# Feed-forward input product by Strassen's seven block products from the fourth slab on

## The reference, cut to what matters

```python
D_FF = 2816
h = x @ w_ffn_in                  # (512, 1024) @ (1024, 2 * 2816)
gate, up = split(h)
x = layer_norm(ALPHA * x + (silu(gate) * up) @ w_ffn_out)
```

## Time and profile before

| what | value |
|---|---|
| median of three runs | 3310.77 us |
| profiled execution, its own time | 3321.89 us |
| its span, first to last instruction | 3320.1 us |
| mean granted TensorE clock | 0.974 of full |
| PE busy | 3131.1 us (94%) |
| DVE busy | 1383.3 us (42%) |
| ACT busy | 1096.3 us (33%) |
| POOL busy | 340.4 us (10%) |

### The profile page before, as it was taken

The page is one execution under the profiler, slowest core; times in us unless marked ns, Lnnn a source line. Parts: engine busy times, 40 slices in busy tenths (PEclk is TensorE's granted clock), DMA queues, the critical chain, the costliest instruction groups (busy, mean ns, idle before and its releaser), DMA issues.

```text
span 3320.1 us, 37603 instructions
## 1 busy us (share of the span) xinstructions
PE 3131.1 (94%) x14830; PEld 2232.9 (67%) x14830; DVE 1383.3 (42%) x1859; ACT 1096.3 (33%) x1831; POOL 340.4 (10%) x266
## 2 busy tenths in 40 slices
PE   6989999979998979999999999998999999999998
PEld 3867777853433338775777688886776677868886
DVE  5676354350211144545334533334554433543333
ACT  3245332231111124455333322213445533232222
POOL 2456020010000001111110000000211110000000
PEclk8988999989999999999999999999999999999999
DMA  6011433448999971110123132233111112322222
GB/s 224 26 51 51 166 138 114 161 194 359 421 421 421 421 247 64 64 53 32 64 70 101 64 102 89 86 92 92 64 52 40 52 63 77 101 77 89 97 84 73
DMA packets 241679, 436.72 MB, mean 132 GB/s; under 512 B 9696, under 2 KB 180192, under 8 KB 216160
## 3 DMA queue, kind: packets, MB, share of 16 engines
q1 hardware_dynamic: 241504, 434.32, 36.2%
HBM read 432.19 MB, written 2.10 MB: 131 GB/s over the span
## 4 chain that ended last, share of the span: by engine, by line
PE 57%; DVE 3%; ACT 2%; DVEq 1%; issue 0%; DMA 0%; ACTq 0%; SPq 0%
PE bank L2314 47%; PE bank L2375 2%; PE bank L2392 2%; PE bank L2411 1%; PE bank L2351 1%; PE bank L1950 1%; DVE ring_r L2644 1%; PE bank L2381 1%; PE bank L2406 1%; ACT ring_r L2511 1%; DVE layers_norm_rstd L1982 1%; DMA ring<-in_w_in 0%; PE bank L2289 0%; DVE layers_negmax L2678 0%; DVEq L2679 0%
## 5 line engine op out<-in xcount | busy, mean ns | idle before, releaser
L2314 PE MATMUL bank<-experts_x_hi_r,ring_r 128*128 128x512 f32 x1720 | 577.4, 401 | 7.0 <-DVE ring_r L2644 7.0
L2314 PE MATMUL bank<-x_r,ring_r 128*128 128x512 f32 x1376 | 546.3, 397 | 0.0
L2644 DVE TENSOR_TENSOR ring_r<-ring,ring_r 128x2048 fp32r<-128x2048 f32 (+2 forms) x162 | 324.4, 2003 | 421.9 <-ACT ring_r L2511 420.7
L2511 ACT ACTIVATE ring_r<-ring 128x2048 fp32r<-128x2048 f32 (+2 forms) x162 | 272.5, 1682 | 477.2 <-PE bank L2314 456.7
L2314 PEld LDWEIGHTS bank<-experts_x_hi_r,ring_r 128*128 128x128 f32 x1720 | 324.3, 189 | 109.9 <-issue 25.7
L2314 PE MATMUL bank<-ring_r 128*128 128x512 f32 (+1 forms) x1224 | 387.5, 377 | 0.0
L2314 PE MATMUL bank<-layers_work_r,ring_r 128*128 128x512 f32 x1312 | 387.0, 396 | 0.0
L2314 PEld LDWEIGHTS bank<-x_r,ring_r 128*128 128x128 f32 x1376 | 259.1, 188 | 63.4 <-issue 1.4
L2823 POOL TENSOR_TENSOR layers_p<-layers_p,layers_recip 128x512 f32<-128x512 f32 (+2 forms) x160 | 145.1, 923 | 1509.2 <-DVEq L2688 1509.2
L2314 PEld LDWEIGHTS bank<-layers_work_r,ring_r 128*128 128x128 f32 x1312 | 245.8, 187 | 68.0 <-issue 7.9
L2314 PEld LDWEIGHTS bank<-ring_r 128*128 128x128 f32 x1224 | 223.7, 188 | 46.7
(11 more groups left out here) (412 smaller groups left out, 4826.4 us busy)
## 6 DMA issues: line engine op xcount, KB each, us to landing
ring<-in_w_in SPq DMA_DIRECT2D x74, 1024.0 KB, 5.1
ring<-in_w_ffn_in SPq DMA_DIRECT2D x44, 1024.0 KB, 5.0
mixer_kept<-in_w_up SPq DMA_DIRECT2D x33, 1024.0 KB, 26.0
mixer_kept<-in_w_down SPq DMA_DIRECT2D x28, 1024.0 KB, 27.0
mixer_kept<-in_w_gate SPq DMA_DIRECT2D x27, 1024.0 KB, 26.6
ring<-in_w_gate SPq DMA_DIRECT2D x24, 1024.0 KB, 26.8
ring<-in_w_down SPq DMA_DIRECT2D x23, 1024.0 KB, 26.0
ring<-in_w_ffn_out SPq DMA_DIRECT2D x32, 704.0 KB, 4.5
```

Of the source, the lines that this page charges most:

```text
L2314: last = pe.matmul(out, lhs, rhs, start=start and k == 0, stop=stop and k == len(pairs) - 1)
L2511: act.activation(r32(whole(key, hi_at(i, key))), whole(key, raw_at(i, key)), ACT.Identity).then_inc(slab_round, 1)
L2644: dve.tensor_tensor(r32(tile), tile, r32(hi), ALU.subtract).then_inc(done, 1)
```

## The change

Slabs 0 to 2 stay as they were. From slab 3 (`PLAIN`) on, the weights are seen as a 2 by 2 arrangement (upper and lower 512 rows; gate and up columns) and the activations as another (upper and lower 512 features; first and last 256 tokens), and the eight block products become seven by Strassen's scheme (in its form with 15 sums). Each of the seven is a chain of 12 matmuls (4 row blocks by 3) with 256 tokens moving.

- The sums of activations (four, `t_hi`/`t_lo`) are made once a layer. VectorE puts high and low part together again (8 additions into `x_whole`), GpSimd makes the four sums, ScalarE rounds them, VectorE makes their low parts.
- The sums of weights are made for each slab. Three go by VectorE (`make_sums`) into `sums_lo`, ScalarE rounds the three (`round_sums`, 128x1536), and VectorE makes their low parts (`rest_of_sums`). A fourth goes by GpSimd in place of the raw up columns (`third`). The raw slab is rounded only after that (`round_quarters`).
- The seven products are put together: ScalarE copies products 1 and 5 out of PSUM; VectorE adds 6 and 7 (`add_sixth_seventh`), 2 and 3 (`make_gate`) and 4 (`make_up`); GpSimd adds twice in between and does the multiplication with SiLU that VectorE did (`multiply`). SiLU now reads and writes SBUF (`gate_curve`).
- The hidden tiles 0 to 5 are rounded and split during slabs 8 to 13, the tiles 6 to 21 only after the last slab, since their places hold the activation sums until then.

The order on each engine within slab f (event `("st", f)`), and the core of the edit:

```diff
-    plan += [e for f in range(KF) for e in (("fg", f), ("fu", f))]
+    plan += [e for f in range(PLAIN) for e in (("fg", f), ("fu", f))] + [("st", f) for f in range(PLAIN, KF)]
+PLAIN = 3
+SEVEN = (1, 5, 6, 7, 2, 3, 4)
+SOON, LATE = 6, 14
...
     # tensor
+                def seven_products(f):
+                    need(("ffn", f))
...
+                    for m in SEVEN:
+                        banks.vacant(pe, ("st", f, m), i)
+                        if m == 5:
+                            sums_split.wait(pe, n + 1)
...
+                        for k in range(4):
+                            b_hi, b_lo = tokens[m][k]
+                            for j, (a, b) in enumerate(((hi, b_hi), (hi, b_lo), (lo, b_hi))):
+                                last = pe.matmul(core.ps(("st", f, m))[:, 0:256], r32(a[:, k, :]), r32(b),
...
     # scalar, for e in plan
                     if e == ("fo", 0):
-                        round_hidden(KF - 1)
+                        gate_curve(KF - 1)
+                        banks.filled(act, ("st", KF - 1, 4), i)
+                        for f in range(SOON, LATE):
+                            round_hidden(f)
...
+                    elif kind == "st":
+                        f = e[1]
+                        if f > PLAIN:
+                            gate_curve(f - 1)
+                        copy_product(f, 1, first_copy)
+                        if f + 1 < KF:
+                            round_sums(f + 1)
+                        copy_product(f, 5, fifth_copy)
+                        if f + 1 < KF:
+                            round_quarters(f + 1)
+                        if f - 8 in range(SOON):
+                            round_hidden(f - 8)
...
     # vector
+                def make_sums(f):
...
+                    dve.tensor_tensor(s1, quarter(i, f, 0, 1), quarter(i, f, 1, 1), ALU.add)
+                    dve.drain().then_inc(first_sum.sem, 1)
+                    dve.tensor_tensor(s2, s1, quarter(i, f, 0, 0), ALU.subtract)
+                    dve.drain()
+                    dve.tensor_tensor(s4, quarter(i, f, 1, 0), s2, ALU.subtract)
+                    dve.drain().then_inc(sums_made.sem, 1)
...
+                    elif kind == "st":
+                        f = e[1]
+                        if f > PLAIN:
+                            make_up(f - 1)
+                        if f + 1 < KF:
+                            make_sums(f + 1)
+                            rest_of_sums(f + 1)
+                        add_sixth_seventh(f)
+                        if f + 1 < KF:
+                            rest_of_slab(("ffn", f + 1))
+                        make_gate(f)
+                        if f - 8 in range(SOON):
+                            rest(hidden(f - 8), hidden_hi(f - 8), hidden_round, i * KF + f - 7, hidden_split)
...
+                    if e == ("fo", 0):
+                        for f in range(LATE, KF):
+                            rest(hidden(f), hidden_hi(f), hidden_round, i * KF + f + 1, hidden_split)
+                    if e == ("fg", 0):
+                        dve.drain()
+                        for k in range(KD):
+                            dve.tensor_tensor(x_whole[:, k, :], r32(x_hi[k]), r32(x[:, k, :]), ALU.add)
+                        dve.drain().then_inc(whole_made.sem, 1)
...
     # gpsimd, after the attention units of the layer
+                whole_made.wait(pool, i + 1)
...
+                def third(f):
+                    first_sum.wait(pool, i * ST + st_no(f) + 1)
...
+                    pool.tensor_tensor(up, quarter(i, f, 0, 0), up, ALU.subtract)
+                    pool.drain().then_inc(third_sum.sem, 1)
+                def multiply(f):
+                    pool.wait_ge(silu_done, i * KF + f + 1)
+                    up_made.wait(pool, i * ST + st_no(f) + 1)
+                    pool.tensor_tensor(hidden(f), side[:, f % 2, :], hidden(f), ALU.mult)
+                    pool.drain().then_inc(hidden_done, 1)
+                third(PLAIN)
+                for f in range(PLAIN, KF):
+                    if f + 1 < KF:
+                        third(f + 1)
+                    if f > PLAIN:
+                        multiply(f - 1)
...
+                    product_copied.wait(pool, 2 * n + 2)
+                    sums_added.wait(pool, n + 1)
+                    pool.tensor_tensor(hidden(f)[:, 256:512], with_seventh(par), fifth_copy(par), ALU.add)
+                    pool.drain()
+                    pool.tensor_tensor(fifth_copy(par), with_sixth(par), fifth_copy(par), ALU.add)
+                    pool.drain().then_inc(fifth_added.sem, 1)
```

More of the change, by code:

```diff
@@ L2156, in layers @@
         elif e[0] != "level":
[L2157 removed]
+            keys += {"norm": lambda: [("mean", e[1]), ("var", e[1])],
+                     "st": lambda: [(*e, r) for r in SEVEN]}.get(e[0], lambda: [e])()
     banks.begin(keys, reps=LAYERS)
@@ L2183, in layers, with quarter @@
     split_no = {k: n for n, k in enumerate(split_keys)}
+    seven = lambda key: key[0] == "ffn" and key[1] >= PLAIN
+    def quarter(i, f, k, n, at=None):
+        base = (raw_at if at is None else at)(i, ("ffn", f))
+        return flat[:, base:base + 2 * KD * P].rearrange("p (k n) -> p k n", k=KD)[:, 4 * k:4 * k + 4, P * n:P * n + P]
     def slabs_of(e):
@@ L2511, in round_slab, with round_sums, round_quarters, gate_curve @@
                     act.activation(r32(whole(key, hi_at(i, key))), whole(key, raw_at(i, key)), ACT.Identity).then_inc(slab_round, 1)
+                def round_sums(f):
+                    n, (lo, hi) = i * ST + st_no(f), both_sums(f % 2)
+                    sums_made.wait(act, n + 1)
+                    if n >= 2:
+                        sums_read.wait(act, n - 1)
+                    act.activation(r32(hi), lo, ACT.Identity).then_inc(sums_round.sem, 1)
+                def round_quarters(f):
+                    third_sum.wait(act, i * ST + st_no(f) + 1)
+                    round_slab(("ffn", f))
+                def gate_curve(f):
+                    gate_made.wait(act, i * ST + st_no(f) + 1)
+                    act.activation(side[:, f % 2, :], side[:, f % 2, :], ACT.Silu)
+                    act.drain().then_inc(silu_done, 1)
+                def copy_product(f, m, dst):
+                    banks.filled(act, ("st", f, m), i)
+                    act.activation(dst(f % 2), core.ps(("st", f, m))[:, 0:256], ACT.Identity).then_inc(banks.done(("st", f, m)), 1)
+                    act.drain().then_inc(product_copied.sem, 1)
                 def round_hidden(f):
@@ L2698, in combine @@
                                              in1=p[:, s, :], op0=ALU.mult, op1=ALU.add).then_inc(combined, 1)
+                def make_sums(f):
+                    n, par, key = i * ST + st_no(f), f % 2, ("ffn", f)
+                    slabs.filled(dve, (i, key))
+                    if n >= 2:
+                        sums_read.wait(dve, n - 1)
+                    s1, s2, s4 = (sum_lo(par, m) for m in range(3))
+                    dve.tensor_tensor(s1, quarter(i, f, 0, 1), quarter(i, f, 1, 1), ALU.add)
[4 more added lines that the diff above has]
+                    dve.drain().then_inc(sums_made.sem, 1)
@@ new lines, in rest_of_sums, with add_sixth_seventh @@
+                def rest_of_sums(f):
+                    lo, hi = both_sums(f % 2)
+                    sums_round.wait(dve, i * ST + st_no(f) + 1)
+                    dve.tensor_tensor(r32(lo), lo, r32(hi), ALU.subtract).then_inc(sums_split.sem, 1)
+                def add_sixth_seventh(f):
+                    n, par = i * ST + st_no(f), f % 2
+                    product_copied.wait(dve, 2 * n + 1)
+                    banks.filled(dve, ("st", f, 6), i)
+                    dve.tensor_tensor(with_sixth(par), first_copy(par), core.ps(("st", f, 6))[:, 0:256], ALU.add)\
+                       .then_inc(banks.done(("st", f, 6)), 1)
+                    banks.filled(dve, ("st", f, 7), i)
+                    dve.drain()
+                    dve.tensor_tensor(with_seventh(par), with_sixth(par), core.ps(("st", f, 7))[:, 0:256], ALU.add)\
+                       .then_inc(banks.done(("st", f, 7)), 1)
+                    dve.drain().then_inc(sums_added.sem, 1)
@@ new lines, in make_gate @@
+                def make_gate(f):
+                    n, par = i * ST + st_no(f), f % 2
+                    dve.wait_ge(hidden_done, i * KF + f - 1)
+                    banks.filled(dve, ("st", f, 2), i)
+                    dve.tensor_tensor(side[:, par, 0:256], first_copy(par), core.ps(("st", f, 2))[:, 0:256], ALU.add)\
+                       .then_inc(banks.done(("st", f, 2)), 1)
+                    fifth_added.wait(dve, n + 1)
+                    banks.filled(dve, ("st", f, 3), i)
+                    dve.tensor_tensor(side[:, par, 256:512], fifth_copy(par), core.ps(("st", f, 3))[:, 0:256], ALU.add)\
+                       .then_inc(banks.done(("st", f, 3)), 1)
+                    dve.drain().then_inc(gate_made.sem, 1)
```

(11 more changed lines are left out.)

98 lines of the change are left out of this document (88 added, 10 removed).

## The result

The kernel after takes 3428.43 us (median of four runs, 3427.45 to 3430.21), the kernel before on the same chips 3310.31 (3306.58 to 3315.31). The ratio is 1.0356 (95% interval 1.0339 to 1.0374): 118 us, 3.6%, slower. The forecast was 3405, in a range from 3320 to 3440. The profiled execution is one of the four, 3427.45 us.

A forecast was written before the change was run, and what follows sets the result against it. TensorE alone was taken to bound the kernel before. Per layer, slabs +38.9, start +4.5, last slab +0.4 and end +3.2 us gave +46.9; two layers, +94 on 3310.8, gave 3405 us, range 3320 to 3440.

The forecast's parts named there:

- TensorE's side: Feed-forward input slabs: 84 matmuls of 256 columns take 9.9 us against 11.2, at most 49 us won.
- The exclusion: VectorE instructions with two SBUF inputs and GpSimd's exclude each other; the later waits, then takes its own time less about 0.15.
- the order of its ties: In each slab, `third` starts before VectorE's second sum, 0.107 against 0.12 us after the first sum, and VectorE is blocked.
- rival 1: VectorE's second sum gets ahead of `third`, or third sum ahead of `multiply`: 1.11 us less a slab, 3367 us; chance 0.22.
- Rival 2: Exclusion bites in part of the slabs or less than counted: periods 11.2 to 12.1, 3320 to 3350 us; chance 0.08.
- Rival 3: GpSimd doesn't block VectorE: chain 10.25 us, 3290 us, or 3270 if VectorE keeps up wholly; chance of faster 0.14.
- The chain: VectorE's stream for one slab, with waits for ScalarE and GpSimd, sets a period of 13.26 us against 11.20 before.
- Start: Before the first seven-product slab, TensorE waits 4.5 us for activation sums, weight sums and low parts, in each layer.
- last slab: Last feed-forward input slab: TensorE's 9.9 us and some 1.7 for the clock, 11.6 against 11.2, so +0.4 a layer.
- end: After the last slab, the first output slab's low part is 0.9 us late, hidden tiles 1.8 and 0.5: sum 3.2.
- TensorE's clock: Lower clock after idle costs at most 2 us a slab, inside the 3.4 us idle, so nothing until the last slab.
- Rivals 4 and 5: No measurable change, the 49 us gain eaten, chance 0.03; clock staying at 1.2 GHz, about 3580 us, 0.03 with slower GpSimd.

The follow-up runs named there:

- experiment 9: Experiment 6's kernel with seven products from slab 4, products added one slab behind, drain releasing `multiply`, ScalarE reordered; 3287.01 us, ratio 0.9916 to the kernel before.
- Experiment 1: Kernel after, with GpSimd's `third` waiting for all three of VectorE's weight sums instead of the first; 3357.96 us, ratio 1.0136 to the kernel before.
- experiment 2: Kernel after, with GpSimd's `third`, `multiply` and second addition shortened, most of that arithmetic left out; 3335.07 us, ratio 1.0066 to the kernel before.
- Experiment 3: Kernel after, with GpSimd's `third`, `multiply` and both additions moved to VectorE; 3351.93 us, ratio 1.0121 to the kernel before.
- experiment 5: Kernel after with Experiment 1's wait, products 5 to 7 added by VectorE during ScalarE's rounding, `multiply` released by a `nop`; 3413.3 us, ratio 1.0302.
- experiment 10: Experiment 5's kernel with a drain in place of the bare instruction that releases `multiply`; 3343.76 us, ratio 1.0088 to the kernel before.
- experiment 6: Experiment 5's kernel with the first output slab's low part and hidden tiles 14 to 21 made earlier; 3407.7 us, ratio 1.0288 to the kernel before.

## Why the prediction was right, and where it was off

**TensorE's side.** 9.9 us a slab were forecast; 84 matmuls take 10.2 from the start of the first to the end of the last, and in experiment 9, where VectorE still sets the distance, slabs are 10.1 apart. Right.

**The exclusion, and the order of its ties.** The second sum, forecast blocked behind `third`, took 1.83, and the third 1.62. GpSimd's second addition was forecast near 2.6, blocked behind the slab's low part; it took 0.73, and it was the first addition that stood blocked, for 2.83. The tie of `third` and the second sum went to GpSimd, by 0.01 us, as in the earlier trace rows, so rival 1 did not come. Experiment 1 makes that rival's case on purpose. Its 3358 lies near the 3367 given for it, but partly by luck: the price was 1.11 us a slab, 38 us, for one instruction in the wait, and the change gave 2.03, 70 us, since `multiply` left VectorE's chain with `third`; the forecast that the 38 were taken from was 23 too low. Rival 2's times don't follow from its periods either: 11.2 to 12.1 a slab would be 3335 to 3366 by the sum above it, not 3320 to 3350; the measured period lies outside. Rival 3 (no blocking) falls with experiment 2, in which the period drops by 2.53 us without a change in VectorE's order. Experiment 3 says the same from the other side: VectorE with all of GpSimd's work is faster by 77 us, so its load didn't make the period 13.70, though the load alone, 11.54, is enough to lose against 11.20. The Trainium skill (SBUF — State Buffer, "Who interferes with whom") says that a VectorE instruction contends with a GpSimd one that reads SBUF if it has two SBUF inputs, and not with at most one. The trace agrees: beside GpSimd those with both inputs in SBUF grew (1.83, 1.62), and those with one in PSUM kept 0.41 (L2854, 2139.91) and 0.42 (L2843 in experiment 9). For GpSimd's own time the prediction gives 1.07 us by its cited rate and a period some 0.5 shorter; over its four terms that would be 0.8, and `third` took 1.30.

**The chain, forecast 13.26, measured 13.70: the term that was mis-sized.** It was too short in three places. From the gate part to the end of the first sum it took 1.46 us against 1.35 (0.21 us of idle time before the sum). From there to the end of the third sum it took 3.65 against 3.58. From product 7 to the gate part, the largest, it took 4.40 against 4.10, by a tie that I gave to the wrong engine: the slab's low part started 0.06 us before the first addition and won. So it took 2.29 where I had 2.15 behind 0.84 of waiting, but both of GpSimd's additions then came after it, and VectorE stood 1.23 us for them. With hidden rests at 0.60 (0.65 forecast) the 18 slabs took 247.67 us where the forecast had 240.5: 7.2 a layer, 14 of the 23 us by which the whole was short. The mechanism came as forecast, but the last term is close in part by luck: the wrong tie made it 0.57 us shorter up to the end of the low part (2.42 against 2.99) and 0.87 longer behind it (1.98 against 1.11), which nearly cancel.

**Start, last slab, end.** The stall before slab 3 was 4.68 us against 4.5. The last slab ran at clock 0.78 and took 12.9, forecast 11.6; 0.99 late after it, forecast 0.9. From the start of the output to the layer's end 131.2 us against 126.9 before: 4.3, forecast 2.3. The idle time of 2.16 is in it. In the 6.1 us behind it the clock was 0.72, and 20 matmuls took them where 4.7 would do by 0.233: 1.4 more, which the forecast had left out. The remaining 0.7 is open. In sum 4.7 + 46.1 + 1.7 + 1.0 + 4.3 = 57.8 us a layer, 59 by the medians, 46.9 forecast.

**TensorE's clock.** In layer 1 it fell in part of the slabs after idle times of 1.9 to 4.1 us and was hidden inside the idle time before the next slab, as forecast: 13.70 and 13.71 at clocks 0.89 and 0.98. Rivals 4 and 5 did not come.

## What to carry to other kernels

Before work goes to GpSimd, write out both engines' streams beside each other: an instruction of GpSimd in the chain of VectorE's SBUF work costs nearly its whole length (1.30 us for 512 columns here) and may cost more than VectorE doing it (0.69), while beside VectorE's PSUM reads or waits it is free. Saving TensorE a tenth of a stage pays in full only when the helpers' chain for one step, waits included, is shorter than the new step, and it loses once that chain is longer than the old one. A way to shorten the chain is to lag the consumers a step (experiment 9), so that VectorE waits for no product that TensorE makes in the same step. Once a stall lies in a loop with TensorE, its clock counts too.

## What the runs showed of the hardware that was not expected

- A semaphore released by a bare instruction of VectorE does not stand for the end of the work ahead of it: in experiment 5 GpSimd started 0.17 us after the start of a 1.76-us instruction that stands ahead of it (2114.64, 2114.47), with a 2.29-us one still to come. In experiment 10, with a drain, it started behind both, for 70 us of difference.
- The engine that started 0.01 us earlier had the tie (GpSimd at 2129.83, VectorE at 2129.84; VectorE at 2137.70, GpSimd at 2137.76), and the loser, whichever engine it is, pays nearly the winner's length.
- Nearly equal idle times before a slab lowered TensorE's clock in one slab and not in another of the same kernel (experiment 6: 0.88 and 1.00; in experiment 5 eleven of 17 slabs were slow, with 2.35 to 2.38 us before all but the first), while 1.28 us before every slab of experiment 10 left it at 1.00.
